# Sixteen-row f32 products replaced by one f32r product over 80 stacked rows, in a decoder step on one core

## The reference, cut to what matters

```
scores = einsum('bihd,bjhd->bhij', q, k) * dmat        # dmat: decay, 0 where j > i
o      = einsum('bhij,bjhe->bihe', scores, v)
S_new  = exp(L*lg) * S + einsum('bjhd,bjhe->bhde', k_dec, v)
```

## Time and profile before

| | |
|---|---|
| median of 3 runs | 787.32 us (786.14 to 787.53) |
| span of the profiled execution | 784.6 us |
| PE busy, of the span | 97% |
| DVE, ACT busy, of the span | 85%, 66% |
| granted TensorE clock, mean | 0.996 |
| PE's share of the chain that ended last | 80% |

### The profile page before, as it was taken

How to read it: one execution, slowest core, us unless ns; L and a number is a source line. 1 busy time by engine, 2 the same in 40 slices (tenths; PEclk the granted TensorE clock), 3 DMA queues, 4 the chain that set the end, 5 groups by cost and what they waited for, 6 DMA issues and landing times.

```text
span 784.6 us, 12128 instructions
## 1 busy us (share of the span) xinstructions
PE 762.0 (97%) x4747; PEld 655.3 (84%) x4747; DVE 667.3 (85%) x903; ACT 513.9 (66%) x641; POOL 97.0 (12%) x120
## 2 busy tenths in 40 slices
PE   8999999999999999999999998999999999999994
PEld 5999999777777699999889975888888888888873
DVE  5699999877878979899977677998889998999897
ACT  7433445775858675345496463878888888887863
POOL 0100001224333200000002001111121111110000
PEclk9999999999999999999999999999999999999998
DMA  9935446599899756455449554999999999999962
GB/s 343 358 133 193 165 168 236 178 330 324 316 326 300 270 185 223 148 176 169 153 165 356 218 215 145 348 365 368 378 367 372 346 381 356 362 374 355 362 261 85
DMA packets 39174, 213.28 MB, mean 272 GB/s; under 512 B 7381, under 2 KB 7637, under 8 KB 19244
## 3 DMA queue, kind: packets, MB, share of 16 engines
q1 hardware_dynamic: 23268, 165.39, 56.8%
q0 software_dynamic: 15408, 45.71, 16.6%
q10 hardware_dynamic: 432, 1.31, 0.4%
HBM read 193.45 MB, written 31.65 MB: 287 GB/s over the span
## 4 chain that ended last, share of the span: by engine, by line
PE 80%; DVE 12%; ACT 4%; DMA 2%; issue 2%; DVEq 0%; ACTq 0%
PE bank L1874 34%; PE bank L1602 30%; DVE w_lo L1101 3%; DVE conv L1148 3%; PE bank L1747 2%; PE bank L1660 2%; PE bank L1713 2%; PE bank L1864 2%; DMA raw<-weights 1%; PE bank L1762 1%; PE bank L1776 1%; PE bank L1783 1%; ACT w_hi L761 1%; PE bank L1904 1%; DMA con<-constants 1%
## 5 line engine op out<-in xcount | busy, mean ns | idle before, releaser
L1602 PE MATMUL bank<-h_hi,w_hi 128*128 128x264 f32 (+1 forms) x640 | 188.7, 295 | 3.6 <-DVE w_lo L1101 3.3
L1602 PE MATMUL bank<-h_lo,w_hi 128*128 128x264 f32 (+1 forms) x640 | 184.0, 287 | 0.0
L1602 PE MATMUL bank<-h_hi,w_lo 128*128 128x264 f32 (+1 forms) x640 | 183.9, 287 | 0.0
L1106 DVE TENSOR_TENSOR ring_lo<-raw,ring_hi 128x2048 fp32r<-128x2048 f32 x72 | 163.6, 2289 | 23.4 <-ACT ring_hi L768 23.4
L1101 DVE TENSOR_TENSOR w_lo<-raw,w_hi 128x1024 fp32r<-128x1024 f32 x112 | 136.9, 1223 | 28.6 <-ACT w_hi L761 28.0
L761 ACT ACTIVATE w_hi<-raw 128x1024 fp32r<-128x1024 f32 x112 | 118.0, 1053 | 55.8 <-PE bank L1602 52.4
L768 ACT ACTIVATE ring_hi<-raw 128x2048 fp32r<-128x2048 f32 x72 | 138.4, 1922 | 19.6 <-PE bank L1874 19.6
L1602 PEld LDWEIGHTS bank<-h_hi,w_hi 128*128 128x128 f32 x640 | 120.4, 188 | 9.5 <-DVE w_lo L1101 5.0
L1602 PEld LDWEIGHTS bank<-h_lo,w_hi 128*128 128x128 f32 x640 | 120.4, 188 | 0.5 <-issue 0.2
L1602 PEld LDWEIGHTS bank<-h_hi,w_lo 128*128 128x128 f32 x640 | 120.2, 188 | 0.0
L1148 DVE SCALAR_TENSOR_TENSOR conv<-u,vec,conv 128x256 f32<-128x256 f32 x240 | 102.0, 482 | 0.6
(11 more groups left out here) (297 smaller groups left out, 1481.1 us busy)
## 6 DMA issues: line engine op xcount, KB each, us to landing
raw<-weights SPq DMA_DIRECT2D x152, 1024.0 KB, 7.0
S_ring<-in_state_ret POOLq DMA_DIRECT2D x20, 512.0 KB, 6.7
out_ret_sample<-S_ring POOLq DMA_DIRECT2D x20, 512.0 KB, 5.8
xT<-in_state_ret POOLq DMA_DIRECT2D x8, 512.0 KB, 5.8
out_ret_sample<-xT POOLq DMA_DIRECT2D x8, 512.0 KB, 7.7
S_five<-in_state_ret POOLq DMA_DIRECT2D x4, 512.0 KB, 6.4
out_ret_sample<-S_five POOLq DMA_DIRECT2D x4, 512.0 KB, 8.8
out_ret_prompt<-S_out POOLq DMA_DIRECT2D x8, 256.0 KB, 4.0
```

What stands on the lines that cost most here:

```text
L1106: dve.tensor_tensor(ring_view(ring_lo, k), raw[raw_slot(NCM + k)][:, :].rearrange("p (k n) -> p k n", k=4), ring_view(ring_hi, k).bitcast( ...
L1602: ins = pe.matmul(out, a[:, k, cols], b[:, k0 + k, :], start=first and k == 0 and j == 0, stop=last and k == ks - 1 and j == 2)
```

## The change

The third product of each feature block in the o block, 16 rows of `v_tok` by 16 x 16 of `P` in f32, becomes one f32r product of `v_two` (80 rows) by a new tensor `P_two` (80 x 16). ACT writes the high part of the 16 x 16 scores to rows 32 and 0 of `P_two`, DVE the low part to rows 64 onward; DVE clears it once. `pick` is widened from 56 to 80 rows, the new rows being zero, so the vb pair reads all 80 rows of `v_two`.

```diff
-        pick = sb("pick", [56, NSAMP], f32r)
+        pick = sb("pick", [80, NSAMP], f32r)
+        P_two = sb("P_two", [80, 16], f32r)
...
-            act.activation(pick[:, :], ident[0:56, 64:72], ACT.Copy).then_inc(pick_ready, 1)
+            act.activation(pick[:, :], ident[0:80, 96:104], ACT.Copy).then_inc(pick_ready, 1)
...
+                        evacuated(act, ("score", h))
+                        if h == 0:
+                            act.wait_ge(two_clear, 3)
+                        for q in (32, 0):
+                            act.activation(P_two[q:q + 16, :], P[0:16, 416:432], ACT.Copy).then_inc(phi_ready, 1)
...
+                    dve.memset(P_two[:, :].bitcast(f32), 0.0).then_inc(two_clear, 1)
...
+                        dve.wait_ge(phi_ready, 2 * h + 2)
+                        dve.tensor_tensor(P_two[64:80, :], P[0:16, 416:432], P_two[0:16, :].bitcast(f32), ALU.subtract).then_inc(plo_ready, 1)
...
+                        pe.wait_ge(vhi_ready, 2 * h + 2)
+                        pe.wait_ge(vlo_ready, h + 1)
                         for et in range(4):
                             b = opened(("o", h, et))
-                            col = 0
-                            for tt, (t0, nt) in enumerate(((0, 128), (128, 128), (256, 16))):
-                                e0 = et * 128
+                            e0, col = et * 128, 0
+                            for tt, (t0, nt) in enumerate(((0, 128), (128, 128))):
                                 f0 = max(t0, NMETA)
-                                ins = pe.matmul(b[:, f0:TP], v_tok[h][0:nt, tt, e0:e0 + 128], P[0:nt, col + f0 - t0:col + TP - t0],
-                                                start=tt == 0, stop=tt == 2)
+                                pe.matmul(b[:, f0:TP], v_tok[h][0:nt, tt, e0:e0 + 128], P[0:nt, col + f0 - t0:col + TP - t0],
+                                          start=tt == 0, stop=False)
                                 col += TP - t0
-                            done(ins)
+                            if et == 0:
+                                pe.wait_ge(plo_ready, h + 1)
+                            done(pe.matmul(b[:, 256:TP], v_two[:, h % 2, e0:e0 + 128], P_two[:, :], start=False, stop=True))
...
-                            done(pe.matmul(b[:, :], pick[:, smp:smp + 1].broadcast_to([56, 128]), v_two[0:56, h % 2, :], start=True, stop=True))
+                            pe.wait_ge(vhi_ready, 2 * h + 2)
+                            done(pe.matmul(b[:, :], pick[:, smp:smp + 1].broadcast_to([80, 128]), v_two[:, h % 2, :], start=True, stop=True))
```

More of the change, by code:

```diff
@@ L473, in build @@
         pick_ready, two_clear, vhi_ready, vlo_ready = sem("pick_ready"), sem("two_clear"), sem("vhi_ready"), sem("vlo_ready")
+        phi_ready, plo_ready = sem("phi_ready"), sem("plo_ready")
         Sp_stored = [sem(f"Sp_stored{i}") for i in range(2)]
```

## The result

| | before | after |
|---|---|---|
| median of the runs | 787.42 us (786.14 to 787.61, 4 runs) | 776.11 us (775.28 to 778.71, 4 runs) |
| ratio, 95% interval | | 0.987 (0.985 to 0.989) |
| span of the profiled execution | 784.6 us | 776.8 us |
| granted TensorE clock of it, mean | 0.996 | 0.989 |

The kernel became 11.3 us faster. The two medians of the same kernel are 1.6 us apart, so a part of the study is on where the scatter is from.

A forecast was written before the change was run, and what follows sets the result against it. PE was taken to bound the kernel from 139 to 357 us. 5.8 (o block) + 3.0 (selector) - 0.07 - 0.3 - 0.1 = 8.3 us off 787.3 gives 779.0 us; range for 8 in 10: 777.6 to 782.0.

The forecast's parts named there:

- The o block, 5.8 us forecast: Mixer's o blocks: 80 rows avoid the 16-row product's drain, saving 1.45 us per head, 5.8 us for four heads.
- The price of the load: The o block's 16-column f32r product over 80 rows: taken as 0.11 us, the time of the next weight load.
- the rival in which the 80-row load is not hidden: o block and vb pairs: exposed loads leave 0.74 against 0.85 us, pairs gain nothing; 786.3 us, no change, chance 0.05.
- The selector, 3.0 us: vb pairs and the unit behind each: 80 rows save 0.18 to 0.19 us a pair, 3.0 us over 16.
- the rival that let it go: Switch ahead of the vb pairs, from the samples' 8-column products, goes too: another 3 us gained, chance 0.04.
- its 776.0: Time forecast by the rival in which the switch ahead of the vb pairs goes too; chance 0.04.
- What is added: Costs of the change: DVE's clearing 0.07 us, head 3's wait 0.3, extra rows 0.1; small ACT and DVE copies covered.
- The 0.3 us that I charged in head 3: Head 3's o block: P_two ready at 247.0 us while PE would come at 246.7, so PE waits.
- The states' loads: Rival, about 152 to 205 us: state loads don't come earlier, 2.8 us of gain lost, 781.8 us; chance 0.10.
- I move both alike: 787.3 - 8.3: Whole kernel: the runs' median, 2.7 us above the profiled span, drops by the same 8.3 us, to 779.0 us.
- 780.9: Upper end of the main forecast's own range, if the 16-column f32r product costs two loads; main forecast's chance 0.77.

The follow-up runs named there:

- e3: The kernel before with only the o block's part of the change, P_two allocated behind qm so that no buffer shifts, pick at 56 rows: 781.02 us.
- e5: The changed kernel with the o block's third product in f32 instead of f32r, still over 80 rows: 780.03 us.
- e6: The changed kernel with the o block's third product in f32r over 16 rows only, low parts left out: 780.71 us.
- e4: The kernel before with only pick and the vb products widened to 80 rows, no P_two, addresses as before: 784.32 us.
- e8: The changed kernel run again, unchanged, six runs: 777.75 us.
- e7: The changed kernel with another unused 64 bytes per partition behind P_two, later buffers 128 bytes further than in the kernel before: 778.66 us.
- e1: The kernel before with one unused tensor of 64 bytes a partition where the change puts P_two: 785.27 us.
- e2: The changed kernel with P_two allocated behind qm, the mixer's last tensor, so that no other buffer moves: 779.61 us.
- e10: The changed kernel with P_two allocated ahead of raw, w_hi and w_lo, so that these shift by 64 bytes too: 777.98 us.

## Why the prediction was right, and where not

**The o block, 5.8 us forecast.** Right, and 0.2 low. The block is 3.06 us where 3.1 was forecast. With the starts of products compared one by one, the blocks of the four heads gave 1.51, 1.51, 1.50 and 1.52 us, 6.0 in all: 0.37 to 0.41 for each of the first three feature blocks, where 0.41 was forecast, and 0.33 for the last, where 0.22 was. e3 has 6.2 us for the part. The price of the load, taken at 0.11 between nothing and 0.22, was right in its middle: e5 adds a second one and pays 0.11 a block.

**The reason was the right one.** The 16 rows stopped the stream, not the f32: e5 and e6. By the rival in which the 80-row load is not hidden, the period would be 1.19 - 0.11 = 1.08 us, and it is 0.79. The Trainium skill's rule that a weight load overlaps a running product only when their row groups differ (TensorE: Matmul & The Clock Gate, Part 3, The mechanism) has no support here: an 80-row load between two 128-row ones starts 0.12 us behind the load ahead. The same section also has a load into the background weight buffer pulled ahead, which the prediction left out; that would fit these rows, and no run here tests it. Its statement on switches of tiling mode (TensorEngine Tiling (Array Packing), Key Properties) agrees with the 16-row rows of e6, 0.28 us for a switch there and back.

**The selector, 3.0 us.** Right. Exits of vb pairs gained 0.18 to 0.20 us, and e4 has 3.1 us. The switch ahead of the pair stayed, as forecast (0.86 us without a load), so the rival that let it go is out. That the first measurement, 776.11 us, met its 776.0 is luck.

**What is added.** The memset has 0.02 us of the chain instead of 0.07. `P_two` takes 0.16 us right behind `k_two` in each head, and PE never waited for it:

```profile
239.95 0.47 DVE L1299 SCALAR_TENSOR_TENSOR k_two<-bank,con,k_two 16x256 fp32r<-16x256 f32 x1
240.35 0.16 DVE L1302 TENSOR_TENSOR P_two<-P,P_two 16x16 fp32r<-16x16 f32 x1
```

The 0.3 us that I charged in head 3 were lost one step earlier, at the vb pair of step 12, where the gain fell by 0.35 us:

```profile
236.61 0.70 PE L1776 MATMUL bank<-v_two,pick 80*128 80x512 f32 x2 [0.27 <-DVE v_two L1273]
```

I had seen that DVE and ACT run without pause there and would become late as PE got ahead, but placed it at the last small operation, not at the first result for which PE waits. The chain of the changed kernel leaves PE at 217.5 us and runs through DVE and ACT to this product. The price was right, the place wrong.

**The states' loads did not pace it in the first profile.** The DMA engines were as busy as in the earlier trace rows, and ACT waited once:

```profile
164.00:198.00 34.00, 34.00 (x222) 26.45 (x221) 26.84 (x46) 25.30 (x47) 13.26 (x20) 1.00 0.93 321
```

```profile
ACT S_ring L790 <- DMA S_ring<-in_state_ret: 1.0, 1, 1.0
```

PE lost nothing by it; stores and with them the loads came earlier as the states' updates did, which the prediction gave as the reason against this rival. In the second profile of the same kernel (e8) it did happen once, behind the last o block. ACT waited for a state, evacuated PE's bank late, and PE stood for 0.74 us:

```profile
244.61 1.06 ACT L790 ACTIVATE xT<-xT 128x1024 f32<-128x1024 f32 x1 [1.85 <-DMA xT<-in_state_ret]
246.09 0.36 PE L1612 MATMUL bank<-h_hi,w_hi 128*128 128x264 f32 x1 [0.74 <-ACT oT L928]
```

The gain fell by 0.9 us there. e7 shows the same with 0.80 us of waiting, the seven other profiles with both parts of the change do not. The rival is out as a price of every run, not as a part of the scatter.

**The step that failed** is the silent one in "I move both alike: 787.3 - 8.3": that everything behind the mixer stays as it was. It does not, since a new tensor moves the buffers allocated behind it. The experts' 1152 products of 512 columns went from 229.0 to 227.5 ns, 1.7 us in the trace and 1.1 to 1.4 us between kernels at equal clock (before and e1, changed and e2 or e10). With the mixer's 8.6, 0.3 more than the forecast's sum, this is the 10.1 us measured at equal clock, to within 0.4 us; the term left out was as large as the whole distance from forecast to range, 1.4 us. The remaining 1.2 us of the 11.3 in the first comparison I put down to few runs with a scattered clock and to slow first runs of the kernel before. That is argued and not shown, since these have no clock listed. The one whose clock is known, the profiled execution, speaks for it: 784.6 us of span at 0.996, where seven later runs at 0.996 have 783.4 to 783.9, and 0.5 us of the difference is the wait for weights shown above. The later six runs, with 9.2 us, lie on the other side of 10.1, and with them the forecast's range would have held, by luck as much as by its terms. The range had no room for the placement or the scatter. It was made from the bounds of the edited instructions alone, and the kernel's own scatter of 3 us between runs was not in it. A slip of its own: 779.0 + 1.8 is 780.8 us, not 780.9, which changes nothing.

## What to carry to other kernels

A short product over few rows between products over 128 costs more by its switch than by its work: look at the loads' starts in a narrow window, and fill its rows up (with parts that are needed anyway, or with zeros) if the tensor is there. Before a forecast that "the rest is unchanged", look at what a new tensor in the middle of the allocations does to the addresses behind it, and when measuring a change that adds one, run it also with the tensor at the end. Where single runs differ in their clock, compare them at equal clock before 1 us is explained.

## What the runs showed of the hardware

- The distance between 512-column f32r products depends on how buffers lie relative to one another: 72 of them took 16.38 us at best, 16.47 to 16.51 with the old places, 16.71 at worst. That is 2%, and shifting all of them by the same 64 bytes changed nothing. Products whose own two operands kept their distance from one another changed too, from 231.0 to 226.7 ns.
- An 80-row weight load among 128-row ones is hidden like theirs (0.12 us behind the load ahead); a 16-row one is not, 0.28 us for the switch there and back.
- A second small weight load, f32 instead of f32r over the same 80 rows and 16 columns, costs 0.11 us.
- The granted clock fell to the lower level for 3.4 us at a time in some executions behind idle times of PE of 1.3 and 1.8 us, and in others, with the same idle times, it did not. Each such stretch cost 0.7 to 1.5 us.
